# Seven adaLN blocks and the first expert gathers of two mixtures, moved and done in two passes

## The reference

```python
for i in range(2):
    sh1, sc1, g1, sh2, sc2, g2 = split(silu(cvec) @ ada_w[i] + ada_b[i], 6)   # for x and for ctx
    hx = rmsnorm(x, norm_g[i, 0]) * (1 + sc1) + sh1
    x = x + g1 * (fourier_mix(hx) if i == 0 else rwkv(hx, hc))
    hx = rmsnorm(x, norm_g[i, 1]) * (1 + sc2) + sh2
    x = x + g2 * ec_moe(hx)          # ctx as well in layer 0
# ec_moe: 16 experts; each takes its top 2 * tokens / 16 tokens by softmax affinity,
# computes (silu(xs @ wg) * (xs @ wu)) @ wd and adds it back, weighted
```

## Time and profile before

| | |
|---|---|
| median of 3 runs | 3915.98 us |
| profiled execution | 3918.93 us, its span 3917.0 us |
| TensorE busy | 3601.0 us (92%) |
| VectorE / ScalarE / GpSimd busy | 1354.0 / 1013.3 / 259.9 us |
| chain that ended last | TensorE 76%, VectorE 8%, DMA 6%, the load queue 4% |
| the two costliest groups, expert products (L892) | 482.0 and 247.3 us of TensorE |
| mean granted TensorE clock | 0.976 of full |

### The profile page before, as it was taken

One profiled execution on the slowest core, in us unless ns is written; L12 is line 12 of the kernel. 1 busy time (PEld: TensorE's weight loads), 2 busy tenths in 40 slices (PEclk: granted clock), 3 DMA queues, 4 the chain that ended last, 5 costly groups with the idle time before them and its releaser, 6 DMA issues.

```text
span 3917.0 us, 63108 instructions
## 1 busy us (share of the span) xinstructions
PE 3601.0 (92%) x28236; PEld 2215.4 (57%) x28236; DVE 1354.0 (35%) x2444; ACT 1013.3 (26%) x1980; POOL 259.9 (7%) x232
## 2 busy tenths in 40 slices
PE   6989999999699989999877887799999999999998
PEld 4555344334357588888342332245558885657886
DVE  2242000001532267776430000026443334545343
ACT  3121111111342255454110000114322222423231
POOL 0000000000000235343100000000000000000000
PEclk9998999999799999999989999999999999999999
DMA  9257988994134343332439999921223222113320
GB/s 334 76 171 277 361 328 328 362 352 165 65 129 153 105 88 82 73 81 66 150 118 378 373 375 387 386 78 49 68 83 96 88 83 87 52 44 97 96 97 22
DMA packets 530974, 666.47 MB, mean 170 GB/s; under 512 B 156600, under 2 KB 299448, under 8 KB 530704
## 3 DMA queue, kind: packets, MB, share of 16 engines
q1 hardware_dynamic: 520592, 633.14, 47.9%
q10 hardware_dynamic: 6912, 18.88, 1.3%
q0 software_dynamic: 3200, 10.42, 0.8%
HBM read 630.92 MB, written 31.46 MB: 169 GB/s over the span
## 4 chain that ended last, share of the span: by engine, by line
PE 76%; DVE 8%; DMA 6%; SPq 4%; ACT 3%; POOL 2%; issue 1%; DVEq 0%; ACTq 0%; POOLq 0%
PE ps L892 13%; PE ps L897 5%; DMA ring<-in_moe_wu 4%; SPq L2999 4%; PE ps L610 4%; PE ps L1096 3%; PE ps L2888 3%; PE ps L2872 3%; PE ps L2871 3%; PE ps L2889 3%; PE ps L2870 3%; PE ps L2887 3%; PE ps L2487 3%; PE ps L2593 3%; PE ps L2211 2%; PE ps L1278 2%
## 5 line engine op out<-in xcount | busy, mean ns | idle before, releaser
L892 PE MATMUL ps<-ring,H 128*64 128x512 f32 x1992 | 482.0, 600 | 52.3 <-DMA ring<-in_moe_wu 39.2
L1002 DVE TENSOR_TENSOR scr<-ps,scr 128x512 f32<-128x512 f32 x32 | 22.1, 692 | 956.5 <-PE ps L897 508.0
L892 PEld LDWEIGHTS ps<-ring,H 128*64 128x64 f32 x1992 | 142.9, 137 | 333.3 <-issue 244.5
L892 PE MATMUL ps<-ring,scr 128*64 128x512 f32 x1024 | 247.3, 599 | 41.5 <-DMA ring<-in_moe_wd 40.1
L2852 DVE TENSOR_TENSOR ring_rounded<-ring,scr_rounded 128x2048 fp32r<-128x2048 f32 x64 | 146.7, 2292 | 218.7 <-ACT scr_rounded L2845 218.3
L2870 PE MATMUL ps<-scr_rounded,ring_rounded 128*128 128x512 f32 x512 | 203.6, 398 | 0.0
L2872 PE MATMUL ps<-scr_rounded 128*128 128x512 f32 x512 | 202.6, 396 | 0.0
L2889 PE MATMUL ps<-scr_rounded 128*128 128x512 f32 x512 | 202.4, 395 | 0.0
L2871 PE MATMUL ps<-H_rounded,scr_rounded 128*128 128x512 f32 x512 | 202.3, 395 | 0.0
L2887 PE MATMUL ps<-scr_rounded,ring_rounded 128*128 128x512 f32 x512 | 201.7, 394 | 0.0
L2845 ACT ACTIVATE scr_rounded<-ring 128x2048 fp32r<-128x2048 f32 x64 | 122.2, 1909 | 244.7 <-PE ps L2889 244.7
(11 more groups left out here) (460 smaller groups left out, 6180.1 us busy)
## 6 DMA issues: line engine op xcount, KB each, us to landing
ring<-in_moe_wd SPq DMA_DIRECT2D x128, 1024.0 KB, 10.8
ring<-in_moe_wu SPq DMA_DIRECT2D x125, 1024.0 KB, 8.5
ring<-in_moe_wg SPq DMA_DIRECT2D x124, 1024.0 KB, 10.0
ring<-in_mlp_w SPq DMA_DIRECT2D x64, 1024.0 KB, 5.4
ring<-in_ada_w SPq DMA_DIRECT2D x48, 1024.0 KB, 11.9
ring<-in_w_in SPq DMA_DIRECT2D x14, 1024.0 KB, 5.2
ring<-in_w_out SPq DMA_DIRECT2D x8, 1024.0 KB, 5.2
st_kka<-scr ACTq DMA_DIRECT2D x16, 384.0 KB, 3.5
```

The costliest lines, as they stand in the source:

```text
L892: ins = pe.matmul(bx[64 * n:64 * n + 64, :], stat_x(k), w[:, k % 4, :], start=k == 0, stop=k == KT - 1)
```

## The change

1. Blocks 41 to 47 leave the first mixture. Their loads come in the plan behind the last down weight of moe0, and their work is in stage n1: two blocks before the sums on TensorE, five after; on ScalarE the five go between the feature tiles of the shift (`behind`). The stage barriers behind moe0 and n1 are taken out.
2. All gathers are done in two passes, gather(0) of moe0 and the four of moe1 too. HTH is made by ScalarE before the experts (in moe0 between the block copies), HTL by GpSimd, not VectorE, in place over HT. Every gather waits for it.
3. HTH of moe1 takes scratch from 14336 to 18432, so only five tiles of moe1 lie apart: the gate tiles of expert 1 and the first down tile of expert 0. Expert 0's gate and up tiles go through the ring.

```diff
-ADA_HEAD, ADA_F1, ADA_F2, ADA_FO, ADA_M0, ADA_TOPK = (0, 8), (8, 16), (16, 24), (24, 28), (28, 31), (31, 48)
+ADA_HEAD, ADA_F1, ADA_F2, ADA_FO, ADA_M0, ADA_TOPK = (0, 8), (8, 16), (16, 24), (24, 28), (28, 31), (31, 41)
+ADA_N1 = (41, 48)
@@ weight_plan
         part("d", NE - 1)
+        if i == 0:
+            ada(*ADA_N1)
@@ phase
-... or name in ("moe1", "fnet", "m0", "post", "m1")):
+... or name in ("moe0", "moe1", "fnet", "m0", "n1", "post", "m1")):
@@ apart
-            [f"wg1.0.{r}.{n}" for r in range(2) for n in range(2)] + ["wu1.0.0.0", "wu1.0.0.1", "wu1.0.1.0"],
-            (8192, 10240, 12288, 14336, 16384, 4096, 6144))}
+            [f"wg1.1.{r}.{n}" for r in range(2) for n in range(2)] + ["wd1.0.0.0"],
+            (8192, 10240, 12288, 4096, 6144))}
@@ shift_scalar(act, tag, segs, behind=None)
                 marks[f"{tag}.h{k}"] = (A_, count[A_])
+                if behind:
+                    behind(k)
@@ gather(q)
-                if i == 0 and q:
-                    ...
-                for k in range(KT):
-                    b = bank(pe, f"xs{i}.{q}.{k}")
-                    for tt in range(4):
-                        ins = pe.matmul(b[:, 0:256], HT[:, tt, k * P:k * P + P], GM_r[:, tt, :].bitcast(F32), ...)
-                    ...
+                if later(pe, f"htl{i}"):
+                    pe.wait_ge(*at(f"htl{i}"))
+                for k in range(KT):
+                    b = bank(pe, f"xs{i}.{q}.{k}")
+                    for lo, w, tts in ((0, 256, range(4)), (256, 128, (4, 5))) if i == 0 else ((0, 256, range(4)),):
+                        for tt in tts:
+                            o = slice(k * P, k * P + P)
+                            pe.matmul(b[:, lo:lo + w], HTL[:, tt, o], GM_r[:, tt, 0:w], start=tt == tts[0], stop=False)
+                            ins = pe.matmul(b[:, lo:lo + w], HTH[i][tt][:, o], GM_r[:, tt, 0:w], start=False, stop=tt == tts[-1])
@@ moe_scalar
+            def rounded(tt):
+                did(A_, act.activation(HTH[i][tt], HT[:, tt, :], ACT.Copy)..., f"hth{i}.{tt}")
+            act.wait_ge(*own(act, A_))
             if i == 0:
-                for b in range(*ADA_TOPK):
+                for n, b in enumerate(range(*ADA_TOPK)):
                     ada_scalar(act, b, b == ADA_TOPK[1] - 1)
+                    if n < ntt:
+                        rounded(n)
+            else:
+                for tt in range(ntt):
+                    rounded(tt)
@@ moe_pool
+            for tt in range(6 if i == 0 else 4):
+                if later(pool, f"hth{i}.{tt}"):
+                    pool.wait_ge(*at(f"hth{i}.{tt}"))
+                did(G_, pool.tensor_tensor(HTL[:, tt, :], HT[:, tt, :], HTH[i][tt].bitcast(F32), ALU.subtract)...)
+            marks[f"htl{i}"] = (G_, count[G_])
@@ stage n1, TensorE
-                    norm_tensor(pe, st, SEGS)
+                    for b in range(*ADA_N1):
+                        if b == ADA_N1[0] + 2:
+                            norm_tensor(pe, st, SEGS)
+                        ada_tensor(pe, b, b == ADA_N1[1] - 1)
@@ stage n1, ScalarE
-                    norm_scalar(act, st, SEGS, True)
+                    ada_scalar(act, ADA_N1[0])
+                    ada_scalar(act, ADA_N1[0] + 1)
+                    root_scalar(act, st, SEGS)
+                    shift_scalar(act, st, SEGS, lambda k: ada_scalar(act, ADA_N1[0] + 2 + k, ...) if ADA_N1[0] + 2 + k < ADA_N1[1] else None)
```

More of the change, by code:

```diff
@@ L201, in build @@
         sems["wkvc"] = semaphore("scan_constants_loaded")
-        for i in range(2, 9):
+        for i in range(2, 7):
             sems[f"x{i}"] = semaphore(f"early_expert_weight_{i}_loaded")
@@ L246, in phase @@
             marks[f"ph.{name}.{e}"] = (e, count[e])
-            if e != "G" and (name[:3] in ("mla", "mix", "wou", "mlp") or name[:2] in ("n2", "n3") or name in ("moe1", "fnet", "m0", "post", "m1")):
+            if e != "G" and (name[:3] in ("mla", "mix", "wou", "mlp") or name[:2] in ("n2", "n3") or name in ("moe0", "moe1", "fnet", "m0", "n1", "post", "m1")):
                 return
@@ L429, in root_scalar, with shift_scalar @@
                 did(A_, act.activation(rs[:, s0:s0 + sn], t[:, 0:sn], ACT.Sqrt if tag in ADA_OF else ACT.Abs_reciprocal_sqrt, bias=eps[:, 0:1], scale=1.0 / D).then_inc(scalar_done, 1), f"free.{tag}.ss{s0}")
-        def shift_scalar(act, tag, segs):
+        def shift_scalar(act, tag, segs, behind=None):
             layer, n = ADA_OF[tag]
@@ L558, in ada_tensor @@
             ada_block(pe, b)
-            if b not in (ADA_HEAD[0], ADA_F1[0], ADA_TOPK[0]):
+            if b not in (ADA_HEAD[0], ADA_F1[0], ADA_TOPK[0], ADA_N1[0]):
                 ada_turn(pe, b - 1)
@@ L776, in build @@
         HTL = S(0, 6, D, of=scr_r)
-        HTH = [S(10240 + D * tt if tt < 4 else 16384 + D * (tt - 4), D, of=scr_r) for tt in range(6)]
+        HTH = [[S(10240 + D * tt if tt < 4 else 16384 + D * (tt - 4), D, of=scr_r) for tt in range(6)],
+               [S(14336 + D * tt, D, of=scr_r) for tt in range(4)]]
         WORK = scr[0:NE, 19200:19200 + TA]
@@ L970, in out @@
                     marks[f"free.dc{i}.{e}"] = (A_, count[A_])
[L971 to L974, removed]
             for e in range(NE):
@@ L994, in experts_vector @@
                     onehot(e // 4 + 1)
[L995 to L998, removed]
                 t = tile(dve, f"ux{i}.{e}")
@@ L3116, in _ @@
                 elif st == "n1":
-                    norm_scalar(act, st, SEGS, True)
+                    ada_scalar(act, ADA_N1[0])
+                    ada_scalar(act, ADA_N1[0] + 1)
+                    root_scalar(act, st, SEGS)
+                    shift_scalar(act, st, SEGS, lambda k: ada_scalar(act, ADA_N1[0] + 2 + k, ADA_N1[0] + 3 + k == ADA_N1[1]) if ADA_N1[0] + 2 + k < ADA_N1[1] else None)
                 elif st == "end":
```

16 lines of the change are left out of this document (2 added, 14 removed).

## The result

The changed kernel takes 3865.68 us (median of 4 runs, 3864.35 to 3869.83), the kernel before 3916.18 beside it on the same chip (4 runs, 3912.24 to 3923.34). The ratio is 0.9871, 95% interval 0.9854 to 0.9888: 50.5 us faster, where 49 were forecast. The profiled execution took 3864.35 (span 3862.5), 54.6 less than that of before.

What follows compares the result with a forecast made beforehand. Transposes queued behind adaLN blocks bound the first mixture, the load stream the second. Terms -23.7, -1.0, -5.3, -12.6 and -6.3 sum to -48.9: 3870.0 profiled, 3867 as median; likeliest case 3860 to 3876, widened to 3853 to 3888.

Steps and rivals of the forecast that it cites:

- Blocks out of the selection: First mixture: with ten blocks left ahead of the transposes, the uncontended gather starts at 292.4 instead of 314.97.
- GpSimd's subtraction: Both mixtures: 2.53 us a tile, twice the 512-column row; the first mixture's six tiles end at 290.7 or later.
- Contention: VectorE ops wait for GpSimd's subtractions: 5.1 us in the first mixture (bounds 0 and 6), 1.1 in the second.
- Gather in two passes: First mixture's gather takes 14.0 us instead of 20.2; the second's takes 10.0, with its experts starting 5.3 earlier.
- n1: Stage n1: moved blocks largely hidden and barrier gone, -1.0 us; bounds -1.2, and +4.5 if nothing is hidden.
- Stream lead: Second mixture: unbroken load stream from 35.7 us after experts' start with 170 tiles left, before 32.0 with 176: -12.6 us.
- Bubbles: Second mixture: shorter third and fourth gathers close load-stream gaps of 3.1 and 3.2 us: -6.3 us.
- No contention: Rival, both mixtures: GpSimd and VectorE slip past each other, 6.2 us less, 3861; chance 0.15.
- all of the selection held: Rival, both mixtures: VectorE's MAX8 and replace wait too, costing about 15 and 9 us, 3885; chance 0.08.
- the lead lost: Rival, second mixture: DMA runs dry again or something else sets the start, so the 12.6 goes, 3880; chance 0.11.
- the blocks without effect: Rival, first mixture: loads, not queue position, set the transposes, so only the faster gather gains, 3884; chance 0.03.
- The slower case: Rival, both mixtures: GpSimd's rounded subtraction far above 2.53 us a tile, all gains eaten at 8.7; chance 0.02.

Runs made afterwards that it cites:

- experiment 1: Kernel before with only the seven blocks moved to n1 and both stage barriers removed; 3892.95 us, ratio 0.9936.
- experiment 9: Experiment 6's kernel with each GpSimd subtraction cut into two of 512 columns; 3861.03 us, ratio 0.9857.
- experiment 7: Changed kernel with the stage barriers behind the first mixture and n1 put back; 3875.75 us, ratio 0.99.
- Experiment 6: Changed kernel with four places apart in the second mixture given out a second time for later expert tiles; 3859.26 us, ratio 0.986.
- Experiment 8: Changed kernel with each of GpSimd's six subtractions of the first mixture made twice; 3878.82 us, ratio 0.9908.
- experiment 2: Changed kernel with all 17 blocks back in the first mixture and the old n1 and barriers; 3885.39 us, ratio 0.9921.

## Why the prediction was right, by its steps

- *Blocks out of the selection.* Right in mechanism and size. Uncontended the gather was to come at 292.4, 23.1 behind the first MAX8; experiment 1 has 22.85.
- *GpSimd's subtraction*, scaled from 512 columns: 2.53 forecast, 2.39 and 2.32 measured, block end 290.7 forecast and 291.1 measured (with a start 1.2 later). The half-size form of experiment 9 takes 1.25, near the 1.28 of the earlier trace rows, and twice that is more than 2.34, the full-size op alone: the scaling counted a cost per op twice.
- *Contention*, the mis-sized term of the first mixture: 5.1 forecast, 3.4 measured (0.85 copy, 0.53 comparison, 2.04 scans). The order of the waits was right; the start times against GpSimd's ops differed by a few tenths, and the wait is a remainder of an op, so such a sum is good to about one op. By the Trainium skill's rule (SBUF — State Buffer, Who interferes with whom) ops with two SBUF inputs contend, and so can a copy and a `tensor_scalar` such as the comparison, in the two-port mode; other one-input ops do not. The rows agree: copy 1.13 and comparison 1.08 against 0.28 and 0.55, MAX8 0.68 in both. In the second mixture 1.1 was forecast and 0.25 measured. The gather at 297.5 came out at 297.41 because a start 1.6 later made up for a contention 1.7 smaller.
- *Gather in two passes.* 14.0 and 10.0 forecast, 13.53 and 9.88 measured. The half-clock start was kept, rightly, at 2.8 and 2.5: the clock is at its lower level up to about 302, and the gathers hold 2.3 and 2.1 above their full-clock pitch.
- *n1.* -1.0 forecast, -1.46 measured, by another path than forecast. The two blocks ahead of the sums were to cost 0.25; in fact the reciprocal starts 4.98 behind the sums instead of 5.78. The shift was to be ready 0.6 ahead of its readers; ScalarE took 15.2 for it (985.25 to 1000.47, "some 14" forecast), and VectorE waited 0.44 once. There is a hidden size in it too: experiment 7 shows that the blocks alone would have cost 8.4 (37.49 against 29.10) and the missing barriers give 9.9 back. My bound of +4.5 for "nothing hidden" was therefore too small.
- *Stream lead.* -12.6 forecast. The first down tile of the third expert is issued at T + 66.05 instead of T + 78.14, 12.1 earlier. It resumed at T + 3.7 (forecast 3.4) and had one dry stretch, as drawn; the 0.5 that is missing is the unbroken stream's start at T + 36.2 instead of T + 35.7. Experiment 6 shows that such a lead reaches the end.
- *Bubbles*, the step that failed in size: -6.3 forecast, -4.6 measured. Behind the third gather's place the lead is 15.8 (the down tiles issued at 2302.01 before and 2248.12 after), 3.7 more. Of the fourth's 3.2 only 0.9 came back. The window at 2264 is full by DMA share and moves 260 GB/s: in both kernels a load from GpSimd's queue (the selectors, 2 x 96 KB) comes at the fourth gather, and takes 4.3 to land before and 6.2 after. Before, it ran where the stream had its bubble; now it seems that the stream pays for it. That reading is from the trace alone, no run moved this load.
- *Rivals.* No contention (3861), and all of the selection held (3885), fall by the VectorE rows above; the lead lost (3880) by the load queue and experiment 6; the blocks without effect (3884) by experiment 1. The slower case needed 8.7 us a tile (8.6 by its own terms). Experiment 8 (5.2 a tile) puts its slope on record: GpSimd's block is 16.7 longer (31.0) and the gather 11.4 later, so some 5 us were free and the rest counted in full.
- *The total.* The parts add up to -50.2 in the profiles and the medians differ by 50.5. That this is within 2 us of the forecast owes something to luck: the stream gave 2.2 less than forecast, the other parts together 3.5 more. The range was drawn a little wider than its terms give (3860 to 3876 and down to 3853, where contention, n1 and clock add up to 3861 to 3873 and down to 3856); nothing hangs on that here. The stage between n1 and the second mixture takes from 954.9 to 962.1 in the profiles of these kernels, though nothing in it was changed: that is the scatter on which one profile pair stands.

## What to carry to other kernels

Ask of each piece of hidden work what it stands in front of on its engine: 17 blocks whose loads were late stood in front of six small transposes, and cost 23 us. Moved work brings its stage borders with it: the blocks were free in their new stage only because two barriers went too (8 us). Where a load stream sets the end, count the tiles that can be issued before each dry stretch; together they are worth the gap they fill at the end (7.5 us in experiment 6, at 2.71 us of stream a tile).

## What the runs showed of the hardware that I had not expected

- In experiment 8 GpSimd and VectorE wait for each other's whole instruction, in both directions: a GpSimd op of 2.37 grew to 3.05 and 3.25 beside a VectorE product and a scan. Cutting GpSimd's op into 2 or 4 didn't lessen the total, since 1024 columns then cost 2.46 and 2.74 us instead of 2.32 (second mixture, where only one VectorE op is beside them), and the longer block meets more VectorE ops.
- With 0.71 us ops back to back on GpSimd, one VectorE comparison was passed over three times (2.36 instead of 0.41).
- The cost of such contention depends on what follows: 3.4 us of it cost nothing in experiment 2, where VectorE had 18 us to wait anyway.
- In the expert loop TensorE fell to its lower clock level for 3 to 4 us, at places that repeat from kernel to kernel, losing 1.7 us each time: once with no idle time ahead (842.6 before), once behind a wait of 2.92 that other kernels have without the fall.
